# Time mix and router: the inverse rows gathered into five stretches, the router's weights loaded ahead of the experts'

## The reference

```python
def step(state, inp):
    r_t, w_t, k_t, v_t, a_t, b_t = inp
    sa = jnp.einsum('bhvk,bhk->bhv', state, a_t)
    state = (state * w_t[:, :, None, :]
             + sa[..., None] * b_t[:, :, None, :]
             + v_t[..., None] * k_t[:, :, None, :])
    y_t = jnp.einsum('bhvk,bhk->bhv', state, r_t)
    return state, y_t
```

```python
group_logits = (hf @ wg_r + bg_r).astype(jnp.float32)
...
exp_logits = (hf @ we_r + be_r).astype(jnp.float32).reshape(n, N_GROUPS, EXPERTS_PER_GROUP)
...
top_val, top_idx = lax.top_k(in_group, TOP_K_IN_GROUP)
...
    hid = jax.nn.silu(xb @ w_gate[e]) * (xb @ w_up[e])
    return hid @ w_down[e]
```

## Time and profile before

| | us |
|---|---|
| median of 3 runs (2602.16 to 2610.34) | 2602.63 |
| the profiled execution | 2609.15 |
| its span in the trace | 2607.0 |
| PE busy | 2239.8 (86%) |
| DVE busy | 1180.0 (45%) |

### The profile page before, as it was taken

The page is one execution under the profiler, slowest core; times in us unless marked ns, Lnnn a source line. Parts: engine busy times, 40 slices in busy tenths (PEclk is TensorE's granted clock), DMA queues, the critical chain, the costliest instruction groups (busy, mean ns, idle before and its releaser), DMA issues. The chain is left out here.

```text
span 2607.0 us, 32570 instructions
## 1 busy us (share of the span) xinstructions
PE 2239.8 (86%) x13812; PEld 1639.9 (63%) x13812; DVE 1180.0 (45%) x1870; ACT 867.9 (33%) x1296; POOL 164.4 (6%) x174
## 2 busy tenths in 40 slices
PE   7999999958997886799999989967985688888875
PEld 7787888846765775587888777756865233333332
DVE  4457565355483565576664343655552311111112
ACT  5344443255663222454442244634232001000000
POOL 0000000000001110000000000001310111111110
PEclk9899999988998877799999999965996799899988
DMA  5122222222111001132222323121104699999996
GB/s 200 65 81 81 97 97 90 94 76 97 65 65 16 16 14 50 64 106 81 97 87 90 114 78 108 49 67 24 51 17 173 269 419 418 416 406 403 402 403 242
DMA packets 107541, 377.26 MB, mean 145 GB/s; under 512 B 55008, under 2 KB 55792, under 8 KB 68736
## 3 DMA queue, kind: packets, MB, share of 16 engines
q1 hardware_dynamic: 85792, 296.44, 31.0%
q10 hardware_dynamic: 9216, 67.11, 6.2%
q0 software_dynamic: 12384, 11.58, 1.5%
HBM read 375.31 MB, written 27.53 MB: 155 GB/s over the span
## 5 line engine op out<-in xcount | busy, mean ns | idle before, releaser
L600 PE MATMUL ps<-xh,wh 128*128 128x512 f32 x1224 | 490.5, 401 | 60.2 <-DVE wl L564 39.5
L601 PE MATMUL ps<-xl,wh 128*128 128x512 f32 x1224 | 485.4, 397 | 0.0
L602 PE MATMUL ps<-xh,wl 128*128 128x512 f32 x1224 | 484.2, 396 | 0.0
L564 DVE TENSOR_TENSOR wl<-raw,wh 128x2048 fp32r<-128x2048 f32 (+2 forms) x123 | 255.2, 2075 | 280.5 <-ACT wh L558 280.5
L3587 PE MATMUL ps<-egu,XT 128*64 128x512 f32 x1088 | 273.8, 661 | 86.3 <-DMA egu<-e_up 82.8
L600 PEld LDWEIGHTS ps<-xh,wh 128*128 128x128 f32 x1224 | 235.0, 192 | 121.9 <-DVE wl L564 46.8
L602 PEld LDWEIGHTS ps<-xh,wl 128*128 128x128 f32 x1224 | 234.8, 192 | 50.5
L601 PEld LDWEIGHTS ps<-xl,wh 128*128 128x128 f32 x1224 | 235.4, 192 | 49.4 <-issue 0.7
L3587 PEld LDWEIGHTS ps<-egu,XT 128*64 128x64 f32 x1088 | 94.9, 151 | 241.8 <-issue 229.3
L558 ACT ACTIVATE wh<-raw 128x2048 fp32r<-128x2048 f32 (+2 forms) x123 | 212.7, 1730 | 90.5 <-PE ps L1079 69.2
L3605 DVE TENSOR_TENSOR HIDT<-ps,SIL 128x256 f32<-128x256 f32 x34 | 14.4, 425 | 353.6 <-ACT SIL L3597 353.6
(11 more groups left out here) (560 smaller groups left out, 3480.5 us busy)
## 6 DMA issues: line engine op xcount, KB each, us to landing
egu<-e_gate SPq DMA_DIRECT2D x68, 1024.0 KB, 14.2
egu<-e_up SPq DMA_DIRECT2D x68, 1024.0 KB, 25.0
ed<-e_down ACTq DMA_DIRECT2D x64, 1024.0 KB, 10.9
raw<-up SPq DMA_DIRECT2D x44, 1024.0 KB, 4.8
raw<-down SPq DMA_DIRECT2D x32, 704.0 KB, 4.1
raw<-rwkv_kr SPq DMA_DIRECT2D x8, 1024.0 KB, 4.8
raw<-in_dn SPq DMA_DIRECT2D x8, 1024.0 KB, 5.0
raw<-sgu_v SPq DMA_DIRECT2D x4, 1024.0 KB, 9.8
```

Of the source, the lines that this page charges most:

```text
L564: e.tensor_tensor(K.WL[s][:, 0:n], K.RAW[r][:, 0:n], K.WH[s][:, 0:n].bitcast(F32), SUB).then_inc(*K.w_low.mark(i))
L600: e.matmul(o, h[:, q, k], x_high[:, k], start=k == 0, stop=False)
L601: e.matmul(o, h[:, q, k], x_low[:, k], start=False, stop=False)
L602: last = e.matmul(o, l[:, q, k], x_high[:, k], start=False, stop=k == KT - 1)
```

## The change

`rows_dve` yields after rows 5, 8, 11 and 13: five stretches (rows 1-5, 6-8, 9-11, 12-13, and 14-15 with the copy), and again 12 steps in all. For group 0, DVE takes only one step of front 1 alone before it weaves the rest with the rows. In `experts_sp` the two router loads stand in front of the ten expert loads, and the wait for "summed" ahead of them is gone.

```diff
-        if n % 2 == 0:
+        if n in (5, 8, 11, 13):
             yield
     e.wait_ge(*K.dve_diag(name, 15, "sum"))
     e.tensor_copy(X[:, 1], X[:, 0].rearrange("p i j -> p j i")).then_inc(*K.dve_diag.mark(name, "both"))
-    yield from nothing(5)
+    yield from nothing(8)
...
     second = front_dve(K, e, 1)
-    for _ in range(6):
-        next(second)
+    next(second)
     weave([second, rows_dve(K, e, 0)], 2)
...
 def experts_sp(K, e):
     for t in K.board.all_at("out2"):
         e.wait_ge(*t)
-    for i in range(2):
-        load_gate_up(K, e, i)
-    for i in range(2, 5):
-        load_gate_up(K, e, i)
-    for t in K.board.all_at("summed"):
-        e.wait_ge(*t)
     e.dma_start(K.RW[:, :, :].rearrange("p k n -> p (k n)"), K.A["router_w"]).then_inc(*K.route_in.landing("weights"))
     e.dma_start(K.RB[:, :], K.A["router_b"]).then_inc(*K.route_in.landing("bias"))
+    for i in range(5):
+        load_gate_up(K, e, i)
```

## The result

The median went from 2602.39 to 2569.91 us, a ratio of 0.9864 (95% interval 0.9848 to 0.988): 32.5 us less, where 31.1 were forecast. The profiled execution took 2571.07 us, with a span of 2568.9.

The account below looks back on a forecast made before the run. Stages with different limits follow one another: a time mix with PE waits, a serial router, full DMA engines from 2085 us. Terms -12.0 - 1.8 - 1.4 - 15.9 = -31.1 from 2602.63 give 2571.5 us, range 2562 to 2584.

Parts of the forecast that it names:

- Group 0's inverses: Time mix, before back 0: rows fit DVE's idle time, PE's wait goes, -12.0 us, and a faster clock gives -1.8.
- The wait is gone: PE in front of back 0: inverses in place at 829.8, PE ready at 830.41, so the 12.10 us wait vanishes.
- The recurrences: Time mix, groups 1 to 3: rows delay the chunks, but DMA waits go and the clock gains; net -1.4 us.
- +4.7 when PE's own products bound it again: Group 1's rows in the recurrence: chunk 2 begins 5.2 us late on PE, gives back 0.46, leaving +4.7.
- The clock's share: Products behind the vanished waits run at a higher clock: about 0.9 us gained in group 1, 1.9 in group 2.
- GpSimd's hold: First rows beside GpSimd's products: DVE held to their ends; unheld, the sum would be 1 us lower.
- Router: Logits start when `XN` ends PE's wait, no longer the bias load; everything after moves along: -15.9 us.
- (a): Groups 1 and 2: later `ST` idles PE, clock rises late, 6 us of work each up to doubled: 2583.5; chance 0.08.
- (b): Expert stage doesn't move with the router, its pace or start set by preloads or tokens' write: 2587; chance 0.05.
- (c): Group 0's inverses arrive no sooner, if DVE waits for `FB` or SP is still busy: 2585; chance 0.06.
- (d): DVE becomes the bound of groups 0 to 2's recurrences, slower than before: 2613.5 at 14 us more each; chance 0.02.
- (e): Time mix better than reckoned, with the recurrences' delays halved: 2565; chance 0.06.

Follow-up runs that it names:

- Experiment 3: The whole change, but rows in pairs (eight stretches) again, group 0 still starting after front 1's first step: 2583.45 us, ratio 0.9929.
- experiment 6: The whole change, but for groups 1 to 3 GpSimd's four masked products wait for chunk 1 of the recurrence: 2575.0 us, ratio 0.9888.
- experiment 1: The kernel before with only the router's loads moved to the front, time mix as before: 2589.36 us, ratio 0.9946.
- experiment 10: The whole change, but for groups 1 to 3 two stretches, rows 1-9 and 10-15 with the copy: 2576.94 us, ratio 0.9884.
- Experiment 2: The whole change, but the router's loads stand behind the experts' again, with the wait for "summed": 2586.3 us, ratio 0.9936.
- experiment 4: The whole change, but five stretches for group 0 alone and rows in pairs for groups 1 to 3: 2577.42 us, ratio 0.9897.
- experiment 9: The whole change, but for groups 1 to 3 six stretches of rows in place of five: 2568.54 us, ratio 0.9856.
- experiment 7: The whole change, but for groups 1 to 3 no rows in the gap between `ST` and the next `RH`: 2571.34 us, ratio 0.9875.
- experiment 5: The whole change, but the router's loads stand behind three experts' (six loads of 1 MB): 2570.67 us, ratio 0.9872.

## Why the prediction was right, step by step

**Group 0's inverses: right.** Forecast -13.8, measured -14.0. The wait fell by 11.8 (12.10 to 0.33; forecast 12.0), the Z products by 1.6 and what follows by 0.7 (forecast 1.8 for both). The five stretches fitted into DVE's idle time; the last filled it to the end and pushed no mask. "The wait is gone" held but for 0.33 us: the chain of 11.25 us was taken as fixed and was 12.17 (the long issue above). In all nine executions in which group 0 has five stretches one of its 16 issues took 0.9 to 1.7 us, in the three others none did; what holds it up the traces don't say. Experiment 3 shows that the early start alone is not enough, and that PE's start follows the copy and the DMAs behind it.

**The recurrences: right in mechanism, about 2 us too little in size** (-1.4 forecast, -3.3 measured, -3.6 by the means of four executions each). The delay was read well at its start: `ST` of chunk 1 +5.3 in group 0's recurrence (forecast +5.2). The step that was mis-sized is "+4.7 when PE's own products bound it again" and its like in the other groups. By the same means, `RH` of chunk 3 came 4.3, 3.3 and 2.9 us later, 10.4 in all, where the sum had 4.7, 4.2 and 3.1, 12.0 in all. The path to it was not the one reckoned: in the profiled execution chunk 2 gave back 2.0 us of the 5.3, not 0.46, and chunk 3 lost 0.9 again.

What came back at the waits was near the forecast: 14.0 where the sum had 13.4. The waits themselves were 10.3 of it. The clock's share shows in the time from the first Z product to the next recurrence. In groups 1 and 2 it was 19.4 to 20.9 us behind a wait and 18.3 without one, a gain of 2.1 and 1.5; in group 3 Z started at 0.50 either way, and that time grew by 0.7 (19.6 to 20.3). Together 3.0, where I had 2.8. The remaining 0.7 of the 14.0 lies ahead of the Z products and has no cause shown.

Whether GpSimd's hold was priced rightly at 1 us of the sum is open, since experiment 6 only moved the hold.

**Router: right**, -15.0 for -15.9, and -15.2 by the medians of experiment 1. The sum counted the wait to `XN`, not the whole 24 us. The 0.9 that is missing lies in front of `XN`: it ended 13.6 us after SP's first issue, not 12.9. The product before it (L658) took 2.08 us in place of 1.32. Around it the granted clock was 0.57 (1946.5 to 1948.0), where it was 0.85 before (1969.5 to 1971.0). In experiment 6 that product took 1.17 us, and the whole stretch to the logits 12.9.

**Rivals.** (a), the clock: in group 0's recurrence it did fall early, see below. The turned keys began 26.8 us into it, where it was 22.2, and the clock was back at 1.00 from 30 us on, where it was from 27. So it rose during the turned keys in both, and the 6 us were not doubled. (b) is refuted by experiment 1, (c) by the copy at 814.78 and L1811's 0.33 us. (d): even two stretches cost 3.5 to 3.8 us a group over five. (e) wanted half the delays; 10.4 of the 12.0 us came.

**What was due to no step.** The profiled spans differ by 38.1 us, 5.6 of it in the first and the sixth stretch of the table, where nothing was edited. The execution profiled before was 6.5 above its median, the one after 1.2 above its own: the two differ by 5.3. That this is what lies there fits, and is argued, not shown.

## What to carry to other kernels

Look for the one instruction that ends a long wait, and count back along its whole chain, DMA issues included: here 11 to 13 us of DMA chain stood behind a single copy, so each microsecond of the copy was one of the end until PE's own work covered it. Don't take such a chain as fixed when the margin is under 1 us. Work that is gathered early in another engine's serial chain delays its first link by more than its end: with two stretches in place of five, `ST` of chunk 0 came 6.0 us later and the recurrence ended 3.8 later (experiment 10). And an edit that is to take a hold away must be looked at in the trace: experiment 6 took 6.3 us of it and brought 5.8 elsewhere. Small loads that the next step needs belong ahead of bulk loads that it doesn't need, and the worth of that is the wait up to the next condition, not the whole wait shown.

## What the runs showed of the hardware

The same instructions can meet the clock at either level. Experiment 2 and the whole change have the same time mix; from 3 to 6 us into group 0's recurrence the clock was 1.00 in the one and 0.50 in the other (windows, columns as in rows 6; first experiment 2, then the whole change):

```profile
846.00:849.00 3.00, 1.69 (x33) 1.38 (x32) 2.79 (x8) 1.18 (x3) 3.00 (x4) 1.00 0.00 0
```

```profile
841.00:844.00 3.00, 3.00 (x36) 2.55 (x34) 2.93 (x5) 0.66 (x2) 3.00 (x4) 0.50 0.00 0
```

In the executions before and of experiments 1, 2, 3, 4 and 9 it stayed at full speed for about 8 us of that recurrence, in experiments 7 and 10 for about 6, and in the whole change (both times) and experiments 5 and 6 it fell after about 2.5. What chooses between them I can't tell from these runs. It cost little here: of the four executions with the same time mix, group 0's recurrence took 55.0 us in experiment 2, and 55.5, 55.3 and 55.6 in the whole change and experiment 5. DVE was the bound of those first chunks: PE waited for chunk 0's `ST` at either clock, 5.71 us in experiment 2 and 4.05 in the whole change, where its own products took longer.

Also unexpected: the time that a small DMA takes depends on more than its size. The write to DRAM of group 0's inverses took 3.9 us once and 2.0 otherwise (experiment 3), one issue of 16 took up to 1.7 us in place of 0.45, and the router's bias took 22.8, 15.3 or 2.7 us by what stood ahead of it.
